# Diagonals of the v rows' weights made one at a time by ScalarE, in a decoder layer on one core

## The chip, the core and the metric

One core of a Trainium2 chip runs the whole layer in one launch. The metric is the device time in microseconds (us), the lower the better. The kernel before takes 3503.22 us, the median of three runs that lie between 3499.84 and 3508.11.

In what follows PE is TensorE (PEld its weight loads), DVE is VectorE, ACT is ScalarE, POOL is GpSimd and SP is SyncE. A line such as L1718 is a line of the kernel before.

## What is computed

The layer has an attention and a convolution branch, and then a PEER channel mixer, which is where the change lies. For each of 1024 tokens PEER picks 128 experts out of 16384 (8 heads, 16 each), takes a row u and a row v of 1024 numbers for each, and adds the v rows up with weights:

```python
    def chunk(xc):
        ...
        u_sel = u_tab[experts]
        act = jax.nn.gelu(jnp.einsum('chkd,cd->chk', u_sel, xc).astype(jnp.float32), approximate=False)
        w = (gates * act).astype(xc.dtype)
        v_sel = v_tab[experts]
        return jnp.einsum('chk,chkd->cd', w, v_sel)
```

The tables are float32, so each token needs 128 u rows and 128 v rows of 4 KB each: 1.07 GB for all tokens.

## The kernel before

The tokens lie in 8 chunks of 128, one token a partition. A first phase projects q, k, v and the convolution's input. In the second phase two things run side by side: the gathers of chunk c, and the front of chunk c + 1 (attention, convolution, the output projection, the queries, the search for the best experts). Its order is written out by hand. A chunk is a pass of 128 slots, and in slot s each engine first does its share of the gathers and then its piece of the front.

The gathers, in slot s of chunk c:

- POOL issues the gather of u row s and that of v row s - 20 (LAG = 20), each an indirect DMA of 128 table rows (512 KB). Each kind has a ring of four buffers (RING = 4), so a gather of u waits for the dot product of the row four before it (`dotted`) and a gather of v for PE's use of the row four before (`row_added`).
- DVE multiplies u row s with the token rows, which lie in PSUM, and sums (L1696, `dot_row`). This gives column s of `dots`.
- ACT takes 16 such columns, a head's, through Gelu (L1530, `gelu`, in slots 0, 16, 32 and so on).
- One slot later (1, 17, 33, ...) DVE multiplies them with the gates (L1708, `weigh_rows`, `weighted`).
- DVE then makes the diagonals: for each row e a 128 x 128 matrix `diag[:, e % 16, :]` with the row's 128 weights on its diagonal and zeros elsewhere. It is the identity times the column of weights. One instruction on 128 x 1024 elements makes eight (L1718, `spread_weights`), in slots 1 and 8 of each 16, so 16 instructions a chunk.
- PE multiplies diagonal and v row and adds into two PSUM banks (L1405, `add_row`, 20 slots behind the dot products). It waits for `diagonal` at every eighth row and for the row's DMA at each.

In chunk 7 five of the last rows (SIDE) are not added by PE but by DVE, after its last dot product (`add_row_aside`, L1727 and L1730).

The front, by slots: attention's eight heads lie in slots 0 to 43, one head in five slots. For each, PE makes the scores, ACT takes them through four activations (L1467 to L1472), DVE runs a scan and a subtraction on each half of the keys (L1603, L1605), ACT an Exp (L1478), PE transposes, ACT copies (L1487) and PE sums (L1363). Beside it DVE does 31 taps of the convolution, four instructions each (L1634). PE's projections follow in slots 49 to 83. The search for the experts is DVE's work alone, in slots 87 to 120 (L1066 to L1166). Chunk 7 has no front beside it.

Chunks 2 to 6 run in a hardware loop on each engine; the others are written out.

## Time and profile before

| | |
|---|---|
| median of three runs | 3503.22 us |
| the profiled execution's own time | 3471.65 us |
| its span | 3469.8 us |
| mean granted clock of TensorE | 0.971 |

The profiled execution is 0.9% below the median of the timed runs. A sum of changes is made against its 3471.65 us and carried over to the median as a difference. What the page calls busy leaves out register and semaphore instructions; POOL's spans are rough. A start or an end of PE's is modelled.

### The profile page before, as it was taken

To read this page: it belongs to the slowest core of one execution; us is meant where nothing else is said; L and a number is where in the kernel's file an instruction comes from. 1 tells how busy PE (TensorE), PEld (TensorE's weight loads), DVE (VectorE), ACT (ScalarE), POOL (GpSimd) and SP (SyncE) were. 2 spreads that over 40 slices of the span, in tenths; PEclk is the share of its full clock that TensorE was granted. 3 is DMA by queue.
4 is the path that set the end of the run, shared out by engine and by line. 5 is a ranking of instruction groups with operands and counts; after the bars stand their busy time and mean duration, and the time that the engine had idled before them with its cause. 6 is when DMAs were issued, how large, how long until landed. Compare 5 with 4: busy or idle time off the path is not lost.

```text
span 3469.8 us, 30029 instructions
## 1 busy us (share of the span) xinstructions
PE 2831.2 (82%) x7929; PEld 1260.8 (36%) x7929; DVE 2348.3 (68%) x5373; ACT 592.7 (17%) x1077; POOL 2027.9 (58%) x2062
## 2 busy tenths in 40 slices
PE   8999488777877998788876988689877988677777
PEld 4445234223432444234432444234432444222222
DVE  2245874987478865988578965978578865944443
ACT  2331210012101420034100420034101420000000
POOL 1000466666666666666666666666666666666664
PEclk9999699999999999999999999999999999999998
DMA  6111899999999999999999999999999999999997
GB/s 217 34 31 58 296 368 353 361 354 361 356 352 362 333 364 344 348 343 354 352 349 346 352 359 352 351 334 354 360 352 343 335 357 353 340 378 372 356 369 279
DMA packets 320480, 1121.68 MB, mean 323 GB/s; under 512 B 36465, under 2 KB 44681, under 8 KB 320296
## 3 DMA queue, kind: packets, MB, share of 16 engines
q0 software_dynamic: 294912, 1073.87, 83.6%
q1 hardware_dynamic: 25384, 45.72, 3.9%
q8 instruction: 71, 1.16, 0.1%
q14 instruction: 113, 0.93, 0.1%
HBM read 1111.01 MB, written 8.45 MB: 323 GB/s over the span
## 4 chain that ended last, share of the span: by engine, by line
PE 22%; DVE 20%; issue 19%; DMA 16%; POOL 7%; another core or an unknown queue 3%; ACT 1%; POOLq 0%; DVEq 0%; ACTq 0%
PE psum L1405 16%; DMA ring_v<-in_peer_v,experts 11%; DVE ring_u L1696 7%; DMA ring_u<-in_peer_u,experts 6%; POOL ring_u L1303 4%; POOL ring_v L1303 4%; DVE acc L1634 2%; PE psum L964 2%; PE psum L1334 1%; PE psum L1363 1%; DVE relu_z L1153 1%; DVE diag L1718 1%; DVE relu_z L1149 1%; PE psum L943 1%
## 5 line engine op out<-in xcount | busy, mean ns | idle before, releaser
L1405 PE MATMUL psum<-ring_v,diag 128*128 128x512 f32 x4076 | 2028.4, 624 | 538.1 <-DMA ring_v<-in_peer_v,experts 455.9
L1696 DVE CUSTOM_DVE_ANT_0 ring_u<-ring_u,psum 128x1024 f32<-128x1024 f32 x1024 | 1241.0, 1215 | 704.0 <-DMA ring_u<-in_peer_u,experts 634.4
L1303 POOL DMA_INDIRECT ring_u<-in_peer_u,experts x1024 | 1005.2, 982 | 797.0 <-DVE experts L1669 351.9
L1303 POOL DMA_INDIRECT ring_v<-in_peer_v,experts x1024 | 1009.0, 985 | 634.1 <-issue 278.8
L1405 PEld LDWEIGHTS psum<-ring_v,diag 128*128 128x128 f32 x4076 | 723.6, 194 | 1589.7 <-DMA ring_v<-in_peer_v,experts 855.6
L478 PE MATMUL psum<-w_sb,xnT 128*128 128x512 f32 x560 | 245.5, 596 | 0.0
L1634 DVE SCALAR_TENSOR_TENSOR acc<-conv_in,taps,acc 128x128 f32<-128x128 f32 x840 | 239.2, 345 | 0.3
L1530 ACT ACTIVATE geld<-dots 128x16 f32<-128x16 f32 x64 | 13.7, 214 | 979.7 <-DVE dots L1696 767.5
L1718 DVE TENSOR_TENSOR diag<-ident,weights 128x1024 f32<-128x1024 f32 x128 | 156.9, 1225 | 7.8 <-issue 2.0
L478 PEld LDWEIGHTS psum<-w_sb,xnT 128*128 128x128 f32 x560 | 106.0, 192 | 126.8 <-issue 123.9
L964 PEld LDWEIGHTS psum<-actT,w_kept 128*128 128x128 f32 x1024 | 130.1, 192 | 52.6 <-issue 46.7
L1603 DVE TENSOR_TENSOR_SCAN log_keep<-log_keep,relu_z 128x512 f32<-128x512 f32 (+1 forms) x96 | 115.7, 1205 | 46.0 <-issue 25.2
L964 PE MATMUL psum<-actT,w_kept 128*128 128x128 f32 x1024 | 131.0, 275 | 4.2 <-ACT actT L1003 4.2
L1334 PE MATMUL psum<-kT,qT 64*128 64x512 f32 (+1 forms) x192 | 108.5, 646 | 7.2 <-DMA qT<-qT_spill 7.2
L943 PE MATMUL psum<-wo_sb,actT 128*128 128x512 f32 x224 | 112.3, 593 | 1.0 <-ACT actT L1523 0.8
L1487 ACT ACTIVATE attT<-psum 128x512 f32<-128x512 f32 (+2 forms) x112 | 58.4, 521 | 311.8 <-PE psum L1350 176.6
L1363 PEld LDWEIGHTS psum<-vals,attT 128*128 128x128 f32 x736 | 94.7, 197 | 34.2 <-issue 33.7
L1363 PE MATMUL psum<-vals,attT 128*128 128x64 f32 x736 | 93.2, 277 | 7.0 <-issue 6.9
L1478 ACT ACTIVATE relu_z<-relu_z 128x512 f32<-128x512 f32 (+1 forms) x96 | 58.2, 608 | 189.6 <-DVE relu_z L1605 142.1
L1350 PE MATMUL psum<-ident,relu_z 128*128 128x128 f32 x368 | 60.1, 277 | 30.7 <-ACT relu_z L1478 22.4
L1696 DVE DVE_READ_ACCUMULATOR2_ANT dots<- 128x1 f32 x1024 | 84.0, 82 | 0.2 <-issue 0.2
L1350 PEld LDWEIGHTS psum<-ident,relu_z 128*128 128x128 f32 x368 | 47.1, 142 | 70.1 <-issue 42.6
(191 smaller groups left out, 1614.6 us busy)
## 6 DMA issues: line engine op xcount, KB each, us to landing
ring_u<-in_peer_u,experts POOLq DMA_INDIRECT x1024
ring_v<-in_peer_v,experts POOLq DMA_INDIRECT x1024
w_sb<-in_w_in SPq DMA_DIRECT2D x4, 2048.0 KB, 19.6
x_in<-in_x SPq DMA_DIRECT2D x8, 512.0 KB, 4.5
w_kept<-in_w_out SPq DMA_DIRECT2D x1, 4096.0 KB, 13.5
h_res<-in_x SPq DMA_DIRECT2D x8, 512.0 KB
w_kept<-in_peer_wq SPq DMA_DIRECT2D x1, 4096.0 KB, 15.2
wo_sb<-in_w_out SPq DMA_DIRECT2D x1, 4096.0 KB, 12.9
```

The costliest lines, as they stand in the source:

```text
L478: last = nc.tensor.matmul(ps[g], xT(i)[:, k, :], w_sb[:, g, k, :], start=k == 0, stop=k == KT_D - 1)
L943: product = nc.tensor.matmul(z[0][:, j * BANK:(j + 1) * BANK], S.actT[:, k, :], wo_sb[:, k, j * BANK:(j + 1) * BANK], start=k == 0, stop=k ...
L964: product = nc.tensor.matmul(z[0][:, h * P:(h + 1) * P], wq_sb[:, k, h * P:(h + 1) * P], S.actT[:, k, :], start=k == 0, stop=k == KT_D - 1)
L1303: nc.gpsimd.indirect_dma_start(ring[kind][:, e % RING, :], None, peer_u[0] if kind == "u" else peer_v[0], bass.IndirectOffsetOnAxis(expert ...
L1334: nc.tensor.matmul(z, qT[lo:lo + HD, a // 2, :], kT[lo:lo + HD, a // 2, lo_key:hi_key], start=True, stop=False)
L1350: last = nc.tensor.transpose(t_ps[:, b * P:(b + 1) * P], S.relu_z[a % 2][:, s:s + P], ident[:, :])
L1363: last = nc.tensor.matmul(o_ps[:, a * HD:(a + 1) * HD], S.attT[:, b, :], vals[:, b, a * HD:(a + 1) * HD], start=n == 0, stop=n == blocks - 1)
L1405: last = nc.tensor.matmul(y_ps[:, j * BANK:(j + 1) * BANK], diag[:, e % TOPK, :], ring["v"][:, e % RING, j * BANK:(j + 1) * BANK], start=F ...
L1603: nc.vector.tensor_tensor_scan(l[:, back], l[:, back], r[:, back], carry, ALU.add, ALU.add).then_inc(S.summed, counts(keys))
L1634: nc.vector.scalar_tensor_tensor(out=acc[:, c, :], in0=conv_in[:, c, t:t + P], scalar=taps[:, c, t:t + 1], in1=acc[:, c, :], op0=ALU.mult, ...
L1696: nc.vector.tensor_tensor_reduce(out=row, in0=row, in1=hn, scale=1.0, scalar=0.0, op0=ALU.mult, op1=ALU.add, accum_out=dots[:, e:e + 1]).t ...
L1718: nc.vector.tensor_tensor(diag[:, at:at + HALF_ROWS, :], spread(ident[:, :], [[0, HALF_ROWS], [1, P]]), spread(weights[:, e:e + HALF_ROWS] ...
```

## The change

ACT makes the diagonals, one a row: 128 a chunk, each the identity through Copy with the row's column of weights as its per-partition scale. Two stand in each of the slots 1 to 8 of every 16. `diagonal` now counts rows, PE waits for it at every row, and each diagonal waits for `row_added` of the row 16 before it, whose place it takes. DVE keeps `weigh_rows`. In chunk 7 the rows of SIDE get no diagonal.

```diff
-    HALF_ROWS = TOPK // 2
+    SPREAD = 1
...
             def add_row(c, e):
 
-                if e % HALF_ROWS == 0:
-                    pe.wait_ge(diagonal, 2 * PH * c + e // HALF_ROWS + 1)
+                is_last = isinstance(c, int) and c == CHUNKS - 1
+                pe.wait_ge(diagonal, pe_rows(e) if is_last else ROWS * c + e + 1)
                 pe.wait_ge(row_in["v"][e % RING], 16 * (FILLS * c + e // RING + 1))
...
+            def spread_weight(c, e):
+
+                is_last = isinstance(c, int) and c == CHUNKS - 1
+                if e % TOPK == 0:
+                    act.wait_ge(weighted, PH * c + e // TOPK + 1)
+                if e >= TOPK or later(c):
+                    act.wait_ge(row_added, pe_rows(e - TOPK) if is_last else ROWS * c + e - TOPK + 1)
+                nc.scalar.activation(diag[:, e % TOPK, :], ident[:, :], ACT.Copy,
+                                     scale=weights[:, e:e + 1]).then_inc(diagonal, 1)
...
+                        h, after = divmod(s, TOPK)
+                        if SPREAD <= after < SPREAD + TOPK // 2 and (h or later(c)):
+                            ch, h = (c, h - 1) if h else (c - 1, PH - 1)
+                            for e in (h * TOPK + 2 * (after - SPREAD), h * TOPK + 2 * (after - SPREAD) + 1):
+                                if not isinstance(ch, int) or ch < CHUNKS - 1 or e not in SIDE:
+                                    spread_weight(ch, e)
...
             gelu(CHUNKS - 1, PH - 1)
+            for e in range(ROWS - TOPK, ROWS):
+                if e not in SIDE:
+                    spread_weight(CHUNKS - 1, e)
...
-                if h or later(c):
-                    dve.wait_ge(diagonal, 2 * (PH * c + h))
+                if later(c):
+                    dve.wait_ge(diagonal, ROWS * (c - 1) + (h + 1) * TOPK)
...
-            def spread_weights(c, e):
-
-                dve.wait_ge(weighted, PH * c + e // TOPK + 1)
-                if isinstance(c, int) and c == CHUNKS - 1 and e == ROWS - HALF_ROWS:
-                    dve.wait_ge(row_added, pe_rows(e - TOPK + HALF_ROWS - 1))
-                elif e >= TOPK or later(c):
-                    dve.wait_ge(row_added, ROWS * c + e - TOPK + HALF_ROWS)
-                at = e % TOPK
-                nc.vector.tensor_tensor(diag[:, at:at + HALF_ROWS, :], spread(ident[:, :], [[0, HALF_ROWS], [1, P]]),
-                                        spread(weights[:, e:e + HALF_ROWS], [[1, HALF_ROWS], [0, P]]),
-                                        ALU.mult).then_inc(diagonal, 1)
...
                             if after == 1:
                                 weigh_rows(ch, h)
-                                spread_weights(ch, h * TOPK)
-                            if after == HALF_ROWS:
-                                spread_weights(ch, h * TOPK + HALF_ROWS)
...
-            spread_weights(CHUNKS - 1, ROWS - TOPK)
             for n, e in enumerate(SIDE):
                 add_row_aside(n, e)
-                if n == 0:
-                    spread_weights(CHUNKS - 1, ROWS - HALF_ROWS)
             end_y()
```

DVE in the loop, slots 97 and 98, before. `u_in2` is the arrival of a u row, `cand` and `top_v` belong to the search.

```order
L1696 ISA ring_u,dots<-ring_u,psum 128x1024 [waits u_in1]
L1696 ISA dots 128x1
L1702 REGISTER_ALU
L1706 REGISTER_ALU [waits gelued]
L1708 TENSOR_TENSOR weights<-geld,gates 128x16 [waits diagonal]
L1716 REGISTER_ALU [waits weighted]
L1718 TENSOR_TENSOR diag<-ident,weights 128x1024 [waits row_added]
L1092 CAST attT<-top_i 128x256 [waits index16]
L1696 ISA ring_u,dots<-ring_u,psum 128x1024 [waits u_in2]
```

The same place after.

```order
L1714 ISA ring_u,dots<-ring_u,psum 128x1024 [waits u_in1]
L1714 ISA dots 128x1
L1720 REGISTER_ALU
L1724 REGISTER_ALU [waits gelued]
L1726 TENSOR_TENSOR weights<-geld,gates 128x16 [waits diagonal]
L1092 CAST attT<-top_i 128x256 [waits index16]
L1714 ISA ring_u,dots<-ring_u,psum 128x1024 [waits u_in2]
```

The instruction of eight diagonals is gone from between the dot product and the search; the multiplication with the gates stays.

ACT in the loop, slots 18 to 20 of the attention, before: the second half's four activations, the copy of the finished chunk to `y_out`, and the Exp of two halves.

```order
L1467 ACTIVATE log_keep_69<-psum 128x512 [waits stick,att_T,z_ready]
L1468 ACTIVATE relu_z_71<-psum 128x512
L1470 ACTIVATE log_keep_69<-log_keep_69 128x512 [waits abs_done]
L1472 ACTIVATE log_keep_69<-log_keep_69 128x512 [waits exp_done]
L1536 REGISTER_ALU [waits row_added]
L1537 ACTIVATE y_out<-psum 128x1024 [waits y_stored]
L1478 ACTIVATE relu_z_71<-relu_z_71 128x512 [waits stick] x2
```

After, from the same activation on.

```order
L1466 ACTIVATE log_keep_69<-psum 128x512 [waits stick,att_T,z_ready]
L1467 ACTIVATE relu_z_71<-psum 128x512
L1469 ACTIVATE log_keep_69<-log_keep_69 128x512 [waits abs_done]
L1471 ACTIVATE log_keep_69<-log_keep_69 128x512 [waits exp_done]
L1538 REGISTER_ALU
L1539 ACTIVATE diag<-ident,weights 128x128 [waits row_added]
L1538 REGISTER_ALU
L1539 ACTIVATE diag<-ident,weights 128x128 [waits row_added]
L1545 REGISTER_ALU [waits row_added]
L1546 ACTIVATE y_out<-psum 128x1024 [waits y_stored]
```

Two diagonals, each with a register operation, now stand ahead of each slot's attention piece; the two shown are those of slot 19.

DVE at the end of chunk 7, before: its weights, eight diagonals, the first row aside, eight diagonals, the other rows aside.

```order
L1708 TENSOR_TENSOR weights<-geld,gates 128x16 [waits diagonal,gelued]
L1718 TENSOR_TENSOR diag<-ident,weights 128x1024 [waits row_added,weighted]
L1727 TENSOR_SCALAR hn_next<-ring_v,weights 128x1024 [waits v_in3]
L1718 TENSOR_TENSOR diag<-ident,weights 128x1024 [waits row_added,weighted]
L1730 SCALAR_TENSOR_TENSOR hn_next<-ring_v,weights,hn_next 128x1024 [waits side_added,v_in3] x4
```

After, these rows read L1726, L1733 and L1736, with no diagonals among them. ACT ends so:

```order
L1529 ACTIVATE geld<-dots 128x16 [waits weighted,dotted]
L1539 ACTIVATE diag<-ident,weights 128x128 [waits row_added,weighted]
L1539 ACTIVATE diag<-ident,weights 128x128 [waits row_added] x11
L1251 UNCONDITIONAL_BRANCH
```

The last eight diagonals no longer stand behind a row aside, which waits for the arrival of its v row.

## Rows read from the trace of the kernel before

**Rows 1.** The page: span, busy time of each engine, DMA.

```profile
span 3469.8 us, 30029 instructions
PE 2831.2 (82%) x7929; PEld 1260.8 (36%) x7929; DVE 2348.3 (68%) x5373; ACT 592.7 (17%) x1077; POOL 2027.9 (58%) x2062
...
DMA  6111899999999999999999999999999999999997
...
q8 instruction: 71, 1.16, 0.1%
q14 instruction: 113, 0.93, 0.1%
```

**Rows 2.** Windows: chunk 4's slots 0-43, 44-87, 88-119, and chunk 7.

```profile
core 0: us, PE busy (x) PEld busy (x) DVE busy (x) ACT busy (x) POOL busy (x), PEclk, DMA share, GB/s
1889.70:2024.51 134.81, 123.06 (x408) 58.03 (x409) 122.22 (x258) 59.96 (x103) 93.37 (x89) 1.00 0.97 357
2024.51:2154.71 130.20, 115.35 (x385) 59.25 (x384) 66.00 (x115) 14.15 (x26) 83.44 (x87) 1.00 0.96 357
2154.71:2251.30 96.59, 68.18 (x131) 23.18 (x129) 91.85 (x275) 3.31 (x5) 63.65 (x66) 0.95 0.94 346
...
3054.36:3420.43 366.07, 261.19 (x511) 89.75 (x510) 175.61 (x280) 2.54 (x8) 241.76 (x252) 0.97 0.96 365
```

**Rows 3.** Windows, L1718 alone (us, DVE busy, clock, DMA): slots 0-43, 88-119.

```profile
1889.70:2024.51 134.81, 7.38 (x6) 1.00 0.97 357
2154.71:2251.30 96.59, 4.89 (x4) 0.95 0.94 346
```

**Rows 4.** Timeline of DVE, chunk 4, slots 97 and 98.

```profile
2187.94 0.17 DVE L1708 TENSOR_TENSOR weights<-geld,gates 128x16 f32<-128x16 f32 x1
2188.24 1.23 DVE L1718 TENSOR_TENSOR diag<-ident,weights 128x1024 f32<-128x1024 f32 x1
2189.38 0.29 DVE L1092 CAST attT<-top_i 128x256 f32<-128x256 uint32 x1
2189.58 1.22 DVE L1696 CUSTOM_DVE_ANT_0 ring_u<-ring_u,psum 128x1024 f32<-128x1024 f32 x1
```

**Rows 5.** Waits of POOL, chunk 4: first slots 0-43, then slots 88-119.

```profile
POOL ring_v L1303 <- PE psum L1405: 10.7, 7, 2.6
POOL ring_u L1303 <- DVE dots L1696: 2.0, 2, 1.7
...
POOL ring_u L1303 <- DVE dots L1696: 9.2, 7, 3.4
POOL ring_u L1303 <- PE psum L1405: 5.5, 2, 3.2
```

**Rows 6.** Groups by form: the removed instruction and ACT's nearest.

```profile
L1718 DVE TENSOR_TENSOR diag<-ident,weights 128x1024 f32<-128x1024 f32 x128 | 156.9, 1225 | 7.8 <-issue 2.0 <-DVE weights L1708 0.5
...
L1509 ACT ACTIVATE actT<-psum,vec 128x128 f32<-128x128 f32 x28 | 8.0, 368 | 34.9 <-remote 19.2 <-PE psum L1385 15.7
...
L1014 ACT ACTIVATE gates_next<-gates_next 128x128 f32<-128x128 f32 x8 | 2.5, 310 | 292.6 <-issue 166.5 <-DVE gates_next L1130 82.8 <-remote 43.3
```

**Rows 7.** Timeline of ACT and DVE, chunk 4, slots 17 to 20.

```profile
1945.19 0.60 ACT L1487 ACTIVATE attT<-psum 128x512 f32<-128x512 f32 x1 [1.56 <-PE psum L1350]
...
1947.31 0.63 ACT L1472 ACTIVATE log_keep<-log_keep 128x512 f32<-128x512 f32 x1
...
1949.46 0.63 ACT L1472 ACTIVATE log_keep<-log_keep 128x512 f32<-128x512 f32 x1
1951.84 1.02 ACT L1537 ACTIVATE y_out<-psum 128x1024 f32<-128x1024 f32 x1 [1.75 <-PE psum L1405]
...
1950.76 1.22 DVE L1603 TENSOR_TENSOR_SCAN log_keep<-log_keep,relu_z 128x512 f32<-128x512 f32 x1
...
1953.75 1.28 DVE L1603 TENSOR_TENSOR_SCAN log_keep<-log_keep,relu_z 128x512 f32<-128x512 f32 x1
```

**Rows 8.** Waits of PE's weight load at the end, 3416 to 3466 us.

```profile
PEld psum L1405 <- DVE diag L1718: 3.8, 1, 3.8
```

**Rows 9.** Timeline of POOL beside DVE, chunk 6, slot 24.

```profile
2740.11 1.97 POOL L1303 DMA_INDIRECT ring_u<-in_peer_u,experts  x1 [0.30 <-issue]
2742.38 0.94 POOL L1303 DMA_INDIRECT ring_v<-in_peer_v,experts  x1 [0.30 <-issue]
...
2740.05 1.22 DVE L1718 TENSOR_TENSOR diag<-ident,weights 128x1024 f32<-128x1024 f32 x1
```

More of the change, by code:

```diff
@@ L1398, in add_row @@
             def add_row(c, e):
-                if e % HALF_ROWS == 0:
-                    pe.wait_ge(diagonal, 2 * PH * c + e // HALF_ROWS + 1)
+                is_last = isinstance(c, int) and c == CHUNKS - 1
+                pe.wait_ge(diagonal, pe_rows(e) if is_last else ROWS * c + e + 1)
                 pe.wait_ge(row_in["v"][e % RING], 16 * (FILLS * c + e // RING + 1))
-                is_last = isinstance(c, int) and c == CHUNKS - 1
                 for j in range(2):
```

## The prediction

> **What bounds the kernel now.** I read the page first, then the stretches of one chunk, then who waits in them. The page says that the 16 DMA engines are busy nine tenths and more from the fifth slice on, that PE is at 82% and DVE at 68% of the span, ACT at 17% [rows 1]. From this alone one would say that the gathers bound everything and that DVE's work is free. The windows say otherwise. Chunk 7, with no front beside it, goes through 128 slots in 366.07 us, 2.86 us a slot, with DVE busy for 175.61 of them: there the gathers set the pace and DVE has slack [rows 2]. Chunk 4, with a front, has three stretches. Slots 0 to 43 take 134.81 us, 3.06 a slot, with DVE busy 91%; slots 44 to 87 take 130.20 us, 2.96 a slot, with DVE busy 51%; slots 88 to 119 take 96.59 us, 3.02 a slot, with DVE busy 95% [rows 2]. DVE is full in the first and the third stretch, and the DMA rate in the third, 346 GB/s, is below chunk 7's 365 [rows 2].
>
> Who sets the pace there is told by POOL, which can issue a gather only when the row four before it is used. In slots 88 to 119 it waited 9.2 us for DVE's dot products and 5.5 us for PE; the dot products follow each other with no gap but their neighbours' work [rows 4, 5]. That stretch is DVE's. In slots 0 to 43 it waited 10.7 us for PE's rows and 2.0 us for DVE's [rows 5]. DVE is full there, but so nearly is PE (123.06 of 134.81 us), and the two are tied to each other through ACT by the attention of each head. That stretch is shared.
>
> **The change part by part.** Removed: 128 instructions of 1.225 us on DVE [rows 6]. They are even through a chunk, 16 in each, but only those in the full stretches count: 6 (7.38 us) in slots 0 to 43 and 4 (4.89 us) in slots 88 to 119 [rows 3].
>
> - Slots 88 to 119. In slot 97 the instruction holds DVE from 2188.24 to 2189.38, 1.14 us, and 0.13 us between the end of the weights and its start go with it [rows 4]. I take 1.2 us, four times, 4.8 us a chunk. The windows allow it: 96.59 less 4.8 is 91.8 us, 2.87 a slot, just above chunk 7's 2.86. I take off a tenth for moments in which a late gather would have stopped DVE anyway: 4.3 us in each of seven chunks (0 to 6), 30 us.
> - Slots 0 to 43. From below nothing, since POOL waits there more for PE; from above all of 7.4 us, since PE's attention pieces wait for DVE's scans. I take half, 3.7 us. Chunk 0 has four such instructions, not six, as it has no weights before slot 17. So 6 x 3.7 and 2.4: 24 us.
> - The others, six in each of those chunks and all 16 of chunk 7: nothing. What hides them is DVE's own slack, 64 of 130 us in the middle stretch and 190 of 366 in chunk 7 [rows 2].
> - The end. PE waited 3.8 us for the last eight diagonals, which stood behind a row aside on DVE [rows 8]. ACT, idle then, makes them directly after the weights. The rows after it are bound by their DMAs in part; I take 3 us, between 0 and 3.8.
>
> Added on ACT: 1019 activations of 128 x 128 from SBUF with a scale per partition. The trace has none of just this kind. The nearest are 310 ns (SBUF, 128 x 128, no scale from memory) and 368 ns (PSUM, with a scale) [rows 6]; I take 340 ns, 5.4 us for each 16, 347 us in all. ACT's share goes from 17% to 27%. In slots 88 to 119 ACT is busy 3.31 of 96.59 us and can't be late [rows 2]. In slots 0 to 43 it is busy 59.96 of 134.81 [rows 2], and 48 diagonals add 16 us. Whether this is late is seen in slots 17 to 20. The two results that DVE's scans need end at 1947.94 and 1950.09, and the scans start at 1950.76 and 1953.75, so there are 2.8 and 3.7 us of slack [rows 7]. Two diagonals (0.7 us) go ahead of the first and four (1.4 us) ahead of the second, and DVE arrives 1.2 us sooner: 0.9 and 1.1 us remain. The copy to `y_out`, for which PE waits at slot 20, had itself waited 1.75 us for PE [rows 7]; six diagonals ahead of it, 2.0 us, use that up. So the chain holds, with little over, and not every slot will be as kind. I take 1 us a chunk, 7 us; from below 0, from above the rival below.
>
> DVE's weights don't wait for ACT's diagonals of the same chunk. ACT now waits at slots 1, 17, ... for `weighted`, and queued behind are its attention pieces of slots 17 and 18. DVE's weights come at the slot's first dot product, and ACT had no earlier work to lose: it was waiting for PE's transposes until 1945.19, at the very time of the weights [rows 7].
>
> Added on PE: a wait at each row instead of each eighth, and a register operation. The diagonal is made at least three slots ahead of its row, as before, and both operations lie ahead of a wait for the row's DMA. Nothing, at most 0.1 us a row where PE streams without a stop.
>
> Added code. In the built program PE's loop body grows from 626 to 834 entries and ACT's from 222 to 479, DVE's shrinks from 786 to 756; with the written-out chunks some 2800 more instructions run. 30029 instructions fetched 2.09 MB [rows 1], 70 bytes each, so 0.2 MB more, 12 packets of 16 KB. One of 16 DMA engines moves 22 GB/s (357 over 16) [rows 2], so a packet takes 0.75 us and can hold up a gather for as long: 9 us at most, I take 6.
>
> **One more term, weighed.** In slot 24 of chunk 6 a gather's issue beside L1718 took 1.97 us, its neighbour 0.94 [rows 9]. One case decides nothing, and I put 0 in the sum; if a third of the 128 cost 1 us each and half of these delayed a gather, it would be 21 us, which the range holds. The Trainium skill (SBUF — State Buffer, "Who interferes with whom" and the summary) says that a DVE operation with two SBUF inputs can block a GpSimd operation that reads SBUF, and that ACT has ports of its own. By that rule the move frees POOL, and the time would be the forecast less those 21 us; the trace agrees in this row.
>
> Against the change speaks another of its rules (Advanced Engine Details and Errata, "The Read-Write Bubble"): ScalarE and VectorE pay a latency between instructions, so use tiles of 512 or 1024 elements. The rows bear this out, since eight times 0.34 is 2.7 us for what took 1.225 [rows 6]. It costs time only where ACT is late, which is the rival below.
>
> **The sum.** -30 - 24 - 3 + 7 + 6 = -44 us. On the profiled execution that is 3471.65 - 44 = 3428 us; on the median 3503 - 44 = 3459 us.
>
> **The rivals.**
>
> - ACT is late in the attention. Speaking for it: the slack of about 1 us that remains in slots 17 to 20 [rows 7], and that ACT works in order, so a late diagonal delays scores, Exp and copies. Against: its 75 idle us in that stretch [rows 2]. If all 48 diagonals land on the chain (16 us a chunk) and only slots 88 to 119 gain (4.3), six chunks lose 11.7 each and the kernel takes 3503 + 70 - 4 (chunk 0) - 3 (the end) = 3566 us. It turns from a gain to a loss at 8.0 us a chunk (4.3 + 3.7), 24 of the 48 diagonals. If it is the case I expect some 34 of them, 11.6 us less 4.3, +44 us, about 3540. Chance 0.10.
> - The gathers take it back. DMA is at 0.94 to 0.97 everywhere [rows 2], and what DVE saves may come back as waits for rows. Against: chunk 7's 2.86 a slot is lower than what remains. It would leave the tail and little else: 3500 us. Chance 0.15.
> - DVE binds the attention too, and POOL is freed. All 7.4 us of slots 0 to 43 (44 in all), 4.8 in slots 88 to 119 (34), 4 at the end and little on the other side: -80 us, 3423. Chance 0.13.
> - The change brings a table load with each group, as Copy stands between Gelu and Exp. The built loop has 12 loads before and after, so this is left at nothing.
>
> My forecast has the remaining 0.62, from 3435 to 3485.
>
> **How the numbers follow.** Within 0.2% (7 us) of the median is what a measurement of this kernel can't tell from no change. Below it lie the forecast (0.62), the third rival (0.13) and a little of the second: 0.76. The second gives the rest, 0.13 for the same. Slower: the first, and a small part of the second, 0.11. The range runs from 3425, near the third rival's 3423, to 3503, the end of no change, and leaves out some 2 in 10.
>
> **What would show it.** DVE's busy time falls by 157 us, ACT's rises by about 350, with a mean near 340 ns. The dot products of slots 97 and 98 lie 1.3 us closer, slots 88 to 119 take about 92 us, and POOL's waits for DVE there shrink. Slots 0 to 43 take about 132 us. Chunk 7 keeps its 366 us. PE's wait for a diagonal at the end is gone. Wrong would be: DVE's scans waiting for ACT's activations by more than a few us a chunk, PE waiting for diagonals or for `y_out`, or the middle stretch growing by what the others lost.

## The result: slower by 0.28%, where 1.3% faster was forecast

The changed kernel takes 3511.14 us (median of 18 runs, 3500.11 to 3520.90), the kernel before 3500.90 us (18 runs, 3488.25 to 3517.53) on the same chip. The ratio is 1.0028, with a 95% interval of 1.0016 to 1.0040. The forecast was 3459 us, its range 3425 to 3503.

The page of the changed kernel: span, busy time of each engine, the sixteen DMA engines in tenths, the two instruction queues, and the chain that ended last.

```profile
span 3507.5 us, 32797 instructions
PE 2820.8 (80%) x7890; PEld 1264.6 (36%) x7929; DVE 2202.5 (63%) x5245; ACT 896.9 (26%) x2096; POOL 1983.5 (57%) x2062
DMA  6111899999999999999999999999999999999998
...
q8 instruction: 73, 1.20, 0.1%
q14 instruction: 137, 1.12, 0.1%
...
PE 22%; DMA 20%; issue 20%; POOL 11%; DVE 10%; another core or an unknown queue 3%; ACT 2%; POOLq 0%; DVEq 0%; ACTq 0%
```

The same chain in the kernel before:

```profile
PE 22%; DVE 20%; issue 19%; DMA 16%; POOL 7%; another core or an unknown queue 3%; ACT 1%; POOLq 0%; DVEq 0%; ACTq 0%
```

VectorE lost 145.8 us of work and ScalarE gained 304.2 [rows 1]: the work moved as the diff says. VectorE's part of the chain that ended last was halved, and the parts of DMA and POOL grew by four points each. The span did not fall. The groups of the same page show where VectorE's time went.

```profile
L1404 PE MATMUL psum<-ring_v,diag 128*128 128x512 f32 x4076 | 2017.6, 621 | 582.4 <-DMA ring_v<-in_peer_v,experts 487.1
L1714 DVE CUSTOM_DVE_ANT_0 ring_u<-ring_u,psum 128x1024 f32<-128x1024 f32 x1024 | 1241.5, 1215 | 848.8 <-DMA ring_u<-in_peer_u,experts 777.0
L1303 POOL DMA_INDIRECT ring_u<-in_peer_u,experts x1024 | 984.9, 962 | 779.8 <-DVE experts L1687 352.9
...
L1539 ACT ACTIVATE diag<-ident,weights 128x128 f32<-128x128 f32 x1019 | 320.4, 388 | 309.6 <-issue 163.5
```

The second row is the dot product. This is its row in the kernel before, and below it the row of the changed kernel in another trace (g1, see below):

```profile
L1696 DVE CUSTOM_DVE_ANT_0 ring_u<-ring_u,psum 128x1024 f32<-128x1024 f32 x1024 | 1241.0, 1215 | 704.0 <-DMA ring_u<-in_peer_u,experts 634.4
...
L1714 DVE CUSTOM_DVE_ANT_0 ring_u<-ring_u,psum 128x1024 f32<-128x1024 f32 x1024 | 1242.5, 1217 | 803.1 <-DMA ring_u<-in_peer_u,experts 730.7
```

VectorE waited for u rows for 634.4 us in the kernel before and 777.0 here, 143 us more. Not all of that is the change's: the trace of the kernel before is of an execution of 3471.65 us and this one of 3509.39, 38 us apart, where the medians differ by 10. g1 took 3477.66 us, and its wait is 96 us longer. In both, time on VectorE turned into waiting on VectorE.

The same stretches as in [rows 2], of the changed kernel: chunk 4's slots 0 to 43, 44 to 87 and 88 to 119, then chunk 7.

```profile
1910.59:2056.64 146.05, 129.30 (x418) 63.22 (x426) 115.77 (x253) 73.56 (x151) 91.04 (x91) 0.95 0.94 338
2056.64:2186.93 130.29, 113.23 (x363) 56.77 (x362) 60.24 (x110) 28.58 (x74) 80.56 (x86) 0.99 0.95 348
2186.93:2282.85 95.92, 67.62 (x134) 24.41 (x132) 87.38 (x270) 13.07 (x37) 61.41 (x64) 0.95 0.97 348
...
3088.29:3460.01 371.72, 261.61 (x513) 91.25 (x512) 157.09 (x265) 42.01 (x135) 236.88 (x253) 0.96 0.95 360
```

VectorE does 4.5 us less in the third stretch, as forecast, but the stretch is only 0.7 us shorter. Chunk 7, in which I expected no change, is 5.7 us longer, and the first stretch 11 us. These are stretches of one chunk in two executions; the table under "Why the prediction was wrong" has all chunks and shows that neither rise is the change's alone. TensorE's granted clock in the first stretch is 0.95, too, where it was 1.00. And yet VectorE's own rows between slots 97 and 98 are as forecast:

```profile
2219.30 0.16 DVE L1726 TENSOR_TENSOR weights<-geld,gates 128x16 f32<-128x16 f32 x1
2219.39 0.28 DVE L1092 CAST attT<-top_i 128x256 f32<-128x256 uint32 x1
2219.59 1.21 DVE L1714 CUSTOM_DVE_ANT_0 ring_u<-ring_u,psum 128x1024 f32<-128x1024 f32 x1
```

From the start of the weights to the next dot product it is 0.29 us, where it was 1.64 [rows 4]: 1.35 us gained in that place. At the end of the stretch most of what four such places gained is gone. The waits of POOL give the first hint of where; the kernel before comes first, the changed kernel second.

```profile
POOL ring_v L1303 <- PE psum L1405: 260.6, 147, 5.1
POOL ring_u L1303 <- DVE dots L1696: 92.2, 91, 4.4
POOL ring_u L1303 <- PE psum L1405: 60.2, 82, 3.5
POOL ring_v L1303 <- remote: 55.5, 25, 4.1
...
POOL ring_v L1303 <- PE psum L1404: 299.6, 148, 5.2
...
POOL ring_v L1303 <- remote: 91.4, 36, 4.1
POOL ring_u L1303 <- DVE dots L1714: 73.8, 81, 4.3
```

Columns: us in total, times, the longest. In both kernels POOL waits nearly 150 times for TensorE's rows ahead of a v gather, over 5 us at the longest, and only 81 to 91 times for VectorE's dot products ahead of a u gather. This was so before the change.

### The profile page after: what moved, and what is told of

It reads as the page before. It is cut to its first block, busy times and chain, and to the rows that moved or that the text cites. A ratio compares the mean times of both kernels' runs of the same rounds, so it can differ in the third digit from the quotient of the medians.

```text
span 3507.5 us, 32797 instructions
## 1 busy us (share of the span) xinstructions
PE 2820.8 (80%) x7890; PEld 1264.6 (36%) x7929; DVE 2202.5 (63%) x5245; ACT 896.9 (26%) x2096; POOL 1983.5 (57%) x2062
## 4 chain that ended last, share of the span: by engine, by line
PE 22%; DMA 20%; issue 20%; POOL 11%; DVE 10%; another core or an unknown queue 3%; ACT 2%; POOLq 0%; DVEq 0%; ACTq 0%
PE psum L1404 16%; DMA ring_v<-in_peer_v,experts 15%; DMA ring_u<-in_peer_u,experts 6%; POOL ring_v L1303 6%; POOL ring_u L1303 5%; DVE ring_u L1714 4%; PE psum L1334 1%; PE psum L943 1%; PE psum L1363 1%; PE psum L964 1%; DVE acc L1652 1%; DVE top_i L1070 1%; DVE relu_z L1073 1%; ACT diag L1539 1%
## 5 line engine op out<-in xcount | busy, mean ns | idle before, releaser
L1714 DVE CUSTOM_DVE_ANT_0 ring_u<-ring_u,psum 128x1024 f32<-128x1024 f32 x1024 | 1241.5, 1215 | 848.8 <-DMA ring_u<-in_peer_u,experts 777.0
L1303 POOL DMA_INDIRECT ring_u<-in_peer_u,experts x1024 | 984.9, 962 | 779.8 <-DVE experts L1687 352.9
L1303 POOL DMA_INDIRECT ring_v<-in_peer_v,experts x1024 | 984.8, 962 | 733.2 <-PE psum L1404 299.6
L1539 ACT ACTIVATE diag<-ident,weights 128x128 f32<-128x128 f32 x1019 | 320.4, 388 | 309.6 <-issue 163.5
L1529 ACT ACTIVATE geld<-dots 128x16 f32<-128x16 f32 x64 | 13.7, 214 | 932.1 <-DVE dots L1714 715.0
```

The costliest lines, as they stand in the source:

```text
L1303: nc.gpsimd.indirect_dma_start(ring[kind][:, e % RING, :], None, peer_u[0] if kind == "u" else peer_v[0], bass.IndirectOffsetOnAxis(expert ...
L1539: nc.scalar.activation(diag[:, e % TOPK, :], ident[:, :], ACT.Copy, scale=weights[:, e:e + 1]).then_inc(diagonal, 1)
L1714: nc.vector.tensor_tensor_reduce(out=row, in0=row, in1=hn, scale=1.0, scalar=0.0, op0=ALU.mult, op1=ALU.add, accum_out=dots[:, e:e + 1]).t ...
```

## The experiments

Eighteen more measurements ran in five sets, each set on one chip beside the kernel before. The chips turned out to differ, so each set names what the kernel before takes on it: 3470.6 us (e), 3265.2 (f), 3466.9 (g), 3261.8 (h), 3470.7 (i). The result above is from a sixth, at 3500.9. I call 3262 to 3265 the quicker chips, the others the slower ones. Ratios are to the kernel before on the same chip unless another kernel is named.

### The parts of the change, one by one (slower chip)

**e1.** TensorE and VectorE skip all diagonals but the first sixteen.

```diff
             def spread_weights(c, e):
+                if later(c) or e >= TOPK:
+                    return
...
-                if e % HALF_ROWS == 0:
-                    pe.wait_ge(diagonal, 2 * PH * c + e // HALF_ROWS + 1)
+                if e % HALF_ROWS == 0 and not later(c) and e < TOPK:
+                    pe.wait_ge(diagonal, e // HALF_ROWS + 1)
```

> Leaves out all diagonals but the first sixteen (the same ones serve every row, so the sums are wrong); no engine makes the others, PE does not wait for them. DVE loses 155 us of work and nothing is added anywhere, the code shrinks a little. Theory D (DVE sets the pace in slots 0 to 43 and 88 to 119, as the forecast had it): 50 to 80 us faster than before, about 3430 to 3450. Theory G (the gathers set the pace everywhere over a stretch of a few slots; DVE's gaps refill as waits for rows): within 10 us of before, 3490 to 3505, and DVE's waits for u rows up by about 150 us.

Measured: 3462.57 us, ratio 0.9984 (0.9969 to 1.0000). VectorE is busy for 2204.9 us as in the changed kernel, and its waits for u rows are 744.0 us. VectorE's relief by itself, with nothing added anywhere, is worth 0.2% here. So most of the forecast gain wasn't eaten by ScalarE's or TensorE's added work: on this chip it wasn't there.

**e2.** ScalarE makes 1008 diagonals into a tile that nobody reads; VectorE's stay. VectorE also waits, once a head, until the sixteen that read the weights it overwrites are made.

```diff
+            def beside(c, e):
+                if e % TOPK == 0:
+                    act.wait_ge(weighted, PH * c + e // TOPK + 1)
+                if later(c) or e > 0:
+                    act.wait_ge(made_aside, ROWS * c + e)
+                nc.scalar.activation(aside[:, :], ident[:, :], ACT.Copy,
+                                     scale=weights[:, e:e + 1]).then_inc(made_aside, 1)
```

> Keeps DVE's diagonals as before and lets ACT make the 128 single ones a chunk as well (but for the last 16), at the same places, into a scratch tile that nobody reads. So it has the change's ACT work and ACT code without its relief of DVE and without PE's waits per row. Theory A (the loss of 10 us comes from ACT being late in the attention, or from its code): 8 to 20 us slower than before. Theory P (the loss comes from PE's waits and PE's code): within 3 us of before.

Measured: 3482.57 us, 1.0029 (1.0014 to 1.0044).

**e3.** TensorE waits at each row; VectorE's instruction counts eight at once.

```diff
-                if e % HALF_ROWS == 0:
-                    pe.wait_ge(diagonal, 2 * PH * c + e // HALF_ROWS + 1)
+                pe.wait_ge(diagonal, ROWS * c + e + 1)
...
-                                        ALU.mult).then_inc(diagonal, 1)
+                                        ALU.mult).then_inc(diagonal, HALF_ROWS)
```

> Before, but DVE's diagonals count by eight and PE waits for its row's count at every row, as after the change. Adds the 96 waits and 112 register operations to PE's loop body, nothing to ACT. Theory P (PE's waits or code cost the 10 us): 8 us or more slower. Theory A: within 3 us of before.

Measured: 3483.57 us, 1.0036 (1.0020 to 1.0051).

**e4.** ScalarE gets two waits a row for what happened long before, and no activations. As in the change, it also waits for `weighted` once in sixteen rows, and that one can be open when ScalarE comes to it.

```diff
+                if e >= TOPK or later(c):
+                    act.wait_ge(row_added, ROWS * c + e - TOPK + 1)
+                act.wait_ge(dotted, ROWS * c + e + 1)
```

> Before, and on ACT at the places of the single diagonals two waits each that have long been fulfilled, with their register operations, but no activation: the added code of ACT and its order of waiting (weights at slot 1 of 16) without the work. If code fetched beside the gathers costs (Theory F), 4 to 10 us slower with 20 or more further packets on the instruction queue; if only ACT's busy time costs (Theory A without the code), within 3 us of before.

Measured: 3475.70 us, 1.0030 (1.0014 to 1.0047); the medians alone differ by 0.15%. The activations of e2 (402.9 us of busy time, 400 ns each) cost no more by these ratios than the waits alone. By the means of twelve runs each, e2 is 3.5 us over e4, a ratio of 1.0010 (0.9994 to 1.0026 by resampling them), so a cost of up to 9 us isn't excluded. In e4's trace ScalarE's queue stands at the wait for `weighted` over 30 times, for 126 us in all, with its attention pieces behind it; no run separates this from the instructions that were added. Each added piece costs some 0.3%, against e1's 0.2%. The pieces don't simply add: e1, e2 and e3 together would be 0.5% slower, and the change is 0.2 to 0.3%.

### Grouped waits, and lighter gathers (quicker chip)

**f1.** The changed kernel, TensorE and ScalarE waiting once in eight rows, four diagonals to a slot.

```diff
-                pe.wait_ge(diagonal, pe_rows(e) if is_last else ROWS * c + e + 1)
+                if is_last and e >= ROWS - LAG:
+                    pe.wait_ge(diagonal, pe_rows(e))
+                elif e % 8 == 0:
+                    pe.wait_ge(diagonal, ROWS * c + min(e + 8, ROWS - LAG) if is_last else ROWS * c + e + 8)
...
-                        if SPREAD <= after < SPREAD + TOPK // 2 and (h or later(c)):
+                        if after in (1, 2, 5, 6) and (h or later(c)):
```

> The changed kernel with its waits taken together: TensorE waits for diagonals once in eight rows, ScalarE waits for added rows once in eight, and makes four diagonals in each of four slots. VectorE still makes none. Against the kernel before. If what the change costs is its added instructions (e3 and e4 each cost 0.3% with waits alone, or nearly), most of that goes and the relief of VectorE stays: ratio 0.998 to 1.001. If the cost is the work of 1024 activations or the handing over from ScalarE to TensorE, it stays at 1.003. If VectorE's relief is worth the 1.2% that I forecast once the waits are out of the way: 0.990.

Measured: 3244.90 us, 0.9938 (0.9923 to 0.9953). I first took this for the groups' doing; g1 and g2 below say otherwise.

**f2.** The kernel before, with 112 more waits a chunk on TensorE, all for the value 1.

```diff
+                else:
+                    pe.wait_ge(diagonal, 1)
```

> The kernel before with the other 112 waits of a chunk on TensorE added as waits for the value 1, fulfilled since the first microseconds, so nothing new is ever waited for and no register is computed for them. If the cost of e3 (0.36%) is that TensorE's stream has more instructions in it: 1.002 to 1.004, with more packets on the instruction queue. If it is that a row waits for a diagonal, or for the arithmetic on the register: 0.999 to 1.001.

Measured: 3266.23 us, 1.0012 (0.9999 to 1.0026): inconclusive, between the two.

**f3 and f4.** Kernel before and changed kernel, with v gathers of half a row; the other half of each place in the ring stays as the first fills left it.

```diff
+                cols = 512 if kind == "v" and (e >= RING or later(c)) else 1024
...
-                    ring[kind][:, e % RING, :], None, peer_u[0] if kind == "u" else peer_v[0],
+                    ring[kind][:, e % RING, 0:cols], None,
+                    peer_u[0] if kind == "u" else peer_v[0] if cols == 1024 else
+                    peer_v[0].rearrange("n (t d) -> (n t) d", t=2),
```

> The kernel before, but each v row's gather fetches 512 of 1024 columns (of other rows; the rest of the ring's row is what the first fills left), so a quarter of the gathered bytes is gone and every instruction stays. If the gathers' bytes bind (the theory that stands after e1): well under the kernel before, 0.90 to 0.96, towards VectorE's and GpSimd's own pace of 2.6 to 2.9 us a slot. If GpSimd's issuing binds and not the bytes: 0.98 to 1.00.

> The changed kernel with the same lighter gathers. To be held against f3. If VectorE's relief was taken back by the gathers' bytes, it shows here: 1.0 to 2.5% under f3 (the 30 to 80 us that VectorE no longer spends where it is the fullest engine), though the change's added instructions cost it 0.3 to 0.6%. If something else than the bytes takes it back (GpSimd's issuing, TensorE's waits): the same as f3 or above it.

Measured: f3 3194.67 us, 0.9774 (0.9752 to 0.9796); f4 3154.32 us, 0.9660 (0.9640 to 0.9680). Between them it is 0.9874 by the medians, 40 us: with lighter gathers the change pays about the 44 us that I had forecast.

### The changed kernel again (slower chip)

**g1** is the changed kernel, **g2** is f1, **g4** is e1. **g3** is the changed kernel with TensorE alone waiting in groups.

```diff
-                pe.wait_ge(diagonal, pe_rows(e) if is_last else ROWS * c + e + 1)
+                if is_last and e >= ROWS - LAG:
+                    pe.wait_ge(diagonal, pe_rows(e))
+                elif e % 4 == 0:
+                    pe.wait_ge(diagonal, min(ROWS * c + e + 4, pe_rows(ROWS - LAG - 1)) if is_last else ROWS * c + e + 4)
```

> The changed kernel itself, once more, beside the kernel before on whatever chip this is: the four light and grouped runs ran on a chip whose kernel before takes 3265 us instead of 3471 to 3501 (382 GB/s in the loop instead of 350). If the ratio of 1.0028 belongs to the change on any chip: 1.002 to 1.004. If quicker transfers let VectorE's relief through, as the lighter gathers did (f4 1.3% under f3): 0.985 to 0.996 on a chip at 3265, and 1.002 to 1.004 on one at 3470 to 3500.

> The grouped kernel of f1 again, beside the changed kernel. If grouping the waits is what brought f1 its 0.9938: 0.5 to 0.8% under g1 on any chip. If it was the chip, and the groups do nothing: the same as g1, within 0.1%.

> The changed kernel with one thing of the grouping: TensorE waits for diagonals once in four rows instead of at each; ScalarE's waits and its slots are as in the change. If the instructions added on TensorE are the cost (e3 0.36% for 112 waits a chunk; 96 of them go here): 0.3% under g1. If ScalarE's are (e4 0.30%): the same as g1, with g2 under both.

> The kernel before with no diagonals made after the first sixteen (e1 again): what VectorE's relief alone is worth on this chip, without any of the change's added work. On a chip at 3470 to 3500: 0.998, as e1. On one at 3265: 0.98 to 0.99 if quicker transfers let the relief through. Either way no kernel that makes its diagonals elsewhere should be under it by more than the interval.

Measured: g1 3473.57 us, 1.0019 (1.0003 to 1.0035). g2 3473.39, 1.0014 (0.9997 to 1.0031). g3 3468.05, 1.0004 (0.9986 to 1.0022). g4 3459.50, 0.9976 (0.9958 to 0.9994). The groups' 0.6% is gone, so it was the chip: g2 and g1 are the same. e1's 0.2% repeats. The change's added work costs 0.4% over g4. g3 is 0.13% under g1, with an interval that reaches zero.

### The quicker kind of chip again

**h1** puts 256 fulfilled waits a chunk on SyncE, **h2** is the changed kernel, **h3** and **h4** are f3 and f4.

```diff
                     store(c - 1)
+                    for e in range(ROWS):
+                        sp.wait_ge(row_added, e + 1)
+                        sp.wait_ge(dotted, e + 1)
```

> The kernel before with 256 waits a chunk that are already fulfilled, on SyncE behind its store of y, where nothing waits behind them but loads needed 300 us later. If e4's 0.3% is what fetching the added code takes from the gathers: 1.002 to 1.004, with more packets on the instruction queues. If it is their place between ScalarE's own work: 0.999 to 1.001.

> The changed kernel on a third chip. If the ratio goes with the speed of the transfers: 1.002 to 1.003 where the kernel before takes 3450 to 3510 us, 0.990 to 0.997 where it takes some 3265. If it doesn't: 1.002 to 1.003 anywhere.

> The kernel before with v gathers of 512 columns. On a chip at 3265 us as f3: 0.977. On one at 3470 to 3500, where more of the time is the gathers': 0.93 to 0.96.

> The changed kernel with the same lighter gathers. If the gathers take VectorE's relief back, then with a quarter of their bytes gone it comes through on any chip: 1.0 to 1.5% under h3, as f4 was under f3 by 1.2%, while h2 beside them stands at 1.002 to 1.003 on a chip at 3470 to 3500. If what lets it through is something else of the quicker chip: 0.2% over h3 on the slower one.

Measured: h1 3261.34 us, 0.9999 (0.9990 to 1.0008). **h2 3239.53, 0.9933 (0.9919 to 0.9946).** h3 3190.67, 0.9783 (0.9764 to 0.9801). h4 3146.34, 0.9647 (0.9634 to 0.9660); h4 to h3 is 0.9861, 44 us. So the same changed kernel is 22 us faster on one chip and 7 to 10 us slower on others. h1 fetched only 3 more packets on its instruction queue than the kernel before (116 against 113), where e4 had fetched 29 more, so it says little on the cost of fetching code.

By now I held that the bytes of the gathers take the relief back, and more so on a chip with slower transfers. The last pair was to show it.

### The theory of the bytes falls (slower chip)

**i1** and **i2** are f3 and f4 with `cols = 256` and `t=4`: v gathers of a quarter row.

> The kernel before with v gathers of 256 of 1024 columns: 37% of the gathered bytes are gone, every instruction stays. On a chip at 3470 to 3500 where the gathers bind: 0.90 to 0.94 (towards some 3180 us, where the half-size gathers brought the quicker chip). On the chip at 3262: 0.970 to 0.978, little under the half-size gathers, since VectorE's and GpSimd's own pace bind there by now.

> The changed kernel with the same gathers. If the bytes take the relief back, it is 1.2 to 1.8% under i1 on any chip: on one at 3470 to 3500 the changed kernel, slower by 0.2 to 0.3% at full bytes, then turns faster. If something else of the slower chips takes it back (their delays in handing over from engine to engine, or fetching the added code): i2 is within 0.3% of i1 there.

Measured: i1 3431.52 us, 0.9898 (0.9881 to 0.9915), where 0.90 to 0.94 was expected. i2 3443.74, 0.9924 (0.9904 to 0.9944); i2 to i1 is 1.0028 by the means of six runs each (1.0012 to 1.0042 by resampling them), where 0.982 to 0.988 was expected. With 37% of the gathered bytes gone the slower chip is hardly quicker, and the change still makes it slower. The page of i1:

```profile
DMA  6111777777767676677777677677767667677775
GB/s 220 34 31 59 267 230 223 225 223 237 230 215 228 222 232 218 217 222 225 224 219 227 217 230 222 216 222 227 223 215 230 215 218 228 218 228 243 229 226 174
```

The DMA engines idle about three tenths of the time, yet chunk 7 takes 359.9 us, against 366.1 with full gathers [rows 2] and 334.8 in h1 with full gathers on the quicker chip.

```profile
2877.71:3212.52 334.81, 254.25 (x514) 87.53 (x512) 175.82 (x281) 2.54 (x8) 245.87 (x253) 0.99 1.02 400
```

## What differs on the slower chips: TensorE's increments arrive late

Laid side by side, chunk 7's slots (from one dot product's start to the next) differ in one thing. On the quicker chip most take 2.56 us, one like the other. On the slower chips the median is 2.56 us as well, but of the 127 slots of the changed kernel 11 take over 4.2 us and 22 more take 3.0 to 4.2; in h2 it is none and 8.

The 2.56 us itself is the gathers' pace. A slot fetches 1.05 MB, in 2.56 us at 410 GB/s, and chunk 7 in h1 ran at 400 GB/s with a DMA share of 1.02. In h2, 93 of the 127 slots take between 2.53 and 2.59 us, with half-row gathers (h4) 6. POOL's own pace is a little quicker: two issues 1.24 us apart, 2.49 us a slot. The changed kernel on the slower chip has 52 slots of 2.53 to 2.59 us, with quarter rows (i1) the kernel before has 13. So bytes set the pace in the undisturbed slots of either chip, and the long slots come on top.

This is one such place in the changed kernel on the slower chip. First TensorE's rows, then POOL's gathers.

```profile
3208.39 1.95 PE L1404 MATMUL psum<-ring_v,diag 128*128 128x512 f32 x4 [0.60 <-issue]
3210.95 1.95 PE L1404 MATMUL psum<-ring_v,diag 128*128 128x512 f32 x4 [0.61 <-DMA ring_v<-in_peer_v,experts]
3213.51 1.95 PE L1404 MATMUL psum<-ring_v,diag 128*128 128x512 f32 x4 [0.61 <-DMA ring_v<-in_peer_v,experts]
...
3210.53 0.94 POOL L1303 DMA_INDIRECT ring_u<-in_peer_u,experts  x1 [0.30 <-issue]
3212.66 0.94 POOL L1303 DMA_INDIRECT ring_v<-in_peer_v,experts  x1 [1.19 <-issue]
3213.91 0.94 POOL L1303 DMA_INDIRECT ring_u<-in_peer_u,experts  x1 [0.31 <-issue]
3218.28 0.94 POOL L1303 DMA_INDIRECT ring_v<-in_peer_v,experts  x1 [3.44 <-PE psum L1404]
```

The v gather at 3218.28 needs the place of the row that TensorE finished at 3212.90 (3210.95 + 1.95). It is issued 5.38 us after that. POOL's wait for `row_added` passed at 3217.51, though the matmuls that count it had long ended. The u gather behind it is held up too, and then TensorE itself runs dry:

```profile
3218.63 1.95 PE L1404 MATMUL psum<-ring_v,diag 128*128 128x512 f32 x4 [0.61 <-DMA ring_v<-in_peer_v,experts]
3222.49 1.96 PE L1404 MATMUL psum<-ring_v,diag 128*128 128x512 f32 x4 [1.90 <-DMA ring_v<-in_peer_v,experts]
3226.26 1.95 PE L1404 MATMUL psum<-ring_v,diag 128*128 128x512 f32 x4 [1.81 <-DMA ring_v<-in_peer_v,experts]
```

The same place of the same kernel on the quicker chip (h2):

```profile
2970.76 1.96 PE L1404 MATMUL psum<-ring_v,diag 128*128 128x512 f32 x4 [0.60 <-DMA ring_v<-in_peer_v,experts]
2973.32 1.96 PE L1404 MATMUL psum<-ring_v,diag 128*128 128x512 f32 x4 [0.60 <-DMA ring_v<-in_peer_v,experts]
...
2973.52 0.94 POOL L1303 DMA_INDIRECT ring_v<-in_peer_v,experts  x1 [0.38 <-DVE dots L1714]
2974.76 0.94 POOL L1303 DMA_INDIRECT ring_u<-in_peer_u,experts  x1 [0.30 <-issue]
2976.09 0.94 POOL L1303 DMA_INDIRECT ring_v<-in_peer_v,experts  x1 [0.38 <-DVE dots L1714]
```

A row ends at 2972.72 and its gather is issued at 2973.52, 0.80 us later; the next ends at 2975.28 and is followed at 2976.09, 0.81 later. POOL's waits for the two rows had passed 0.04 us after their ends.

I worked this out for the first 1000 waits for `row_added` of each profile: when POOL's wait passed, less the later of the row's recorded end and the passing of POOL's wait before it plus 0.57 us, which is its usual distance.

| kernel, chip | over 1 us late | their sum, us | latest, us |
|---|---|---|---|
| before (an execution of 3471.65 us) | 109 | 330 | 4.6 |
| changed (3500.9) | 148 | 451 | 4.8 |
| e1, g4: no diagonals (3470.6, 3466.9) | 144, 130 | 398, 389 | 4.6, 4.8 |
| e2, e3, e4 (3470.6) | 134, 131, 139 | 395, 375, 387 | 4.8, 4.6, 4.7 |
| g1: changed; g2, g3: grouped (3466.9) | 160; 140, 154 | 436; 403, 443 | 4.5; 4.4, 4.7 |
| i1, i2: quarter gathers (3470.7) | 151, 151 | 540, 564 | 7.2, 6.8 |
| f1 to f4, h1 to h4 (3265.2, 3261.8) | none | 0 | 0.3 |

On the quicker chips not one of 8000 waits is late by more than 0.3 us. On the slower ones 11 to 16% are. The trace shows it from the other side too: in i1 three increments of `row_added` stand at 3136.66, 3136.72 and 3136.78, though TensorE's record of a row is 1.95 us long and no two rows start closer than 1.72 us. Increments closer than 0.25 us occur 69 to 125 times a run on the slower chips and never on the quicker. Three in a row occur only with the quarter gathers. VectorE's `dotted` shows one such pair at most, and POOL's waits for it are over 1 us late 21 to 30 times (44 to 73 us in all) on the slower chips and 14 to 16 times (29 to 35 us) on the quicker. So it is TensorE's increments above all. The ends of matmuls are modelled in the trace, so it may be that the row is finished late rather than reported late; for the gather that waits it is the same.

One more thing divides the traces the same way. On the slower chips they hold only 706 to 743 of the 1019 increments of `row_added`, and 18060 to 22581 semaphore updates in all; on the quicker ones none is missing of `row_added`, and it is 42670 to 43567 in all. So the close pairs are counted in an incomplete record. The lateness itself is taken from POOL's waits and TensorE's rows, which are as complete in the one kind as in the other (1016 and 1019). Whether the lost records and the late increments have one cause, and whether the recording has a part in it, no run here can tell.

Late waits and long slots go together. In chunk 7 of the changed kernel on the slower chip, a wait over 1 us late lies at most 8 us before each of the 11 slots of over 4.2 us, and before fewer than half (40) of the 86 slots under 2.7. The lateness there is 68 us in all, and the chunk takes 46.6 us more than 127 slots of 2.56. In h2 there is none, and it takes 9.0 more.

The chips' difference of some 205 us fits in size: 330 to 450 us of lateness with full gathers, a part of which the ring of four rows covers. The sums don't put the kernels in order, though. i1 has 540 us of it and is 39 us quicker than the kernel before, and e1 has more of it than e3 and is 21 us quicker.

That the lateness goes with the chip is shown by traces on four slower chips and two quicker ones. That it is what makes them slower is argued from i1 and from the sums; no experiment took the lateness away. Why it occurs is open.

## Why the prediction was wrong, step by step

One chunk in one execution says little. This table has, from the starts of the dot products, the stretches summed over chunks 0 to 6, and chunk 7, in us. Each line is one trace. e1 and g4 are one kernel, and so are the two changed ones at 3509 and g1: 9 to 11 us between such a pair are no effect.

| kernel (its execution) | slots 0-43 | 44-87 | 88-119 | chunk 7 |
|---|---|---|---|---|
| before (3471.65) | 938.2 | 910.0 | 675.9 | 366.1 |
| changed (3509.39) | 960.5 | 912.0 | 679.9 | 371.7 |
| g1, changed (3477.66) | 949.7 | 901.9 | 677.4 | 364.9 |
| e1, no diagonals (3461.24) | 939.3 | 902.2 | 669.0 | 363.4 |
| g4, no diagonals (3469.44) | 930.4 | 908.4 | 673.6 | 365.6 |
| h1, before, quicker chip (3262.10) | 886.0 | 816.6 | 643.0 | 334.8 |
| h2, changed, quicker chip (3238.18) | 872.3 | 820.2 | 629.3 | 334.1 |

- **Reading what bounds the kernel.** This is the step that failed. I read a DMA share of 0.94 to 0.97 and chunk 7's 2.86 us a slot as the steady pace of the gathers [rows 2]. (The DMA engines are at nine tenths from the sixth slice on, not the fifth [rows 1]; nothing hangs on it.) It is the mean of slots of 2.56 us, which the gathers do set, and of pauses in which POOL waits for a late increment of TensorE's. i1 shows that the bytes are the smaller part: 37% fewer, 6 us less in chunk 7 (on another chip of the slower kind). And I read slots 88 to 119 as VectorE's, from 95% busy and POOL's 9.2 us of waits for it, and so priced the relief at 54 us in two stretches. Measured, the relief alone gives 0.16% and 0.24% on the slower chips, 6 to 8 us (e1, g4). In that stretch VectorE has work queued after a pause and catches up in the next one; a pause that comes from TensorE absorbs what VectorE saves. That last sentence is argued, not measured by itself.
- **-30 us, slots 88 to 119.** On the quicker chip about half of the term is there. The third stretch of chunk 4 in h1 (kernel before, plus SyncE's waits) and in h2 (changed), one below the other:

```profile
2039.89:2131.64 91.75, 65.69 (x133) 22.70 (x132) 91.18 (x275) 3.31 (x5) 62.56 (x64) 0.98 0.98 367
...
2023.74:2112.71 88.97, 65.68 (x134) 22.92 (x132) 86.97 (x271) 13.06 (x37) 61.61 (x64) 0.98 0.99 382
```

  VectorE is busy for 91.18 of 91.75 us there, and the stretch loses 2.8 us; over seven chunks it is 13.7. On the slower chips the change saved nothing there (675.9 us before, 677.4 and 679.9 after), and leaving the diagonals out saved 2 to 7 us, no more than two traces of one kernel differ by.
- **-24 us, slots 0 to 43.** From h1 to h2 it is 13.7 us, a little over half. On the slower chips the changed kernel is over the kernel before here, by 12 us in g1 and 22 in the first trace. On one and the same chip g1 has 19 us more here than g4, which has no diagonals at all, while all of g1 costs 14 to 15 us over g4. So the added work costs most where the attention is, if a single pair of traces can be trusted that far.
- **Nothing elsewhere.** True on the quicker chip, within 4 us in the middle stretch and 1 in chunk 7. On the slower ones too: chunk 7's 5.7 us more in the first trace aren't the change's, since g1 has 364.9 against 366.1.
- **-3 us, the end.** TensorE's weight loads wait for diagonals for 0.5 us in the last 67 us, where they waited 3.8 [rows 8]. The wait went as forecast. From the last dot product to the end it is 47.5 us after 49.4 on the slower chips, but 48.0 after 47.8 on the quicker.
- **+7 us, ScalarE late.** The activation is 388 ns each by the page and 314 ns of busy time (320.4 over 1019), against my 340. e2 costs no more than e4 within the noise, so little of the cost is the activations' own work. But TensorE waits 76.3 us in weight loads and 18.4 us in matmuls for diagonals, for which I had put nothing; in f1, with four diagonals a slot, matmuls wait 2.6 us for them. g2 shows that this made no difference on the slower chip, and in h2, which gains, the two waits are 112.5 and 17.6 us.
- **+6 us, added code, and TensorE's waits at nothing.** Instruction packets rose by 26 and 0.23 MB, the bytes that I had estimated in twice as many packets. What came with them cost more: 0.30% in e4 and 0.36% in e3, some 10 to 12 us each, and 0.4% together. On a quicker chip constant waits, without register operations, cost 0.12% (f2), with an interval from -0.01% to 0.26%. Whether the code, the register operations, the waits or ScalarE's stand at `weighted` cost this on the slower chips isn't settled. The lateness table offers 45 to 65 us more of late increments in e2 to e4 than in the kernel before, but this is one profile each, and e1 has as much more and gains.
- **POOL freed.** POOL's busy time fell from 2027.9 us [rows 1] to 1983.5, 44 us, and a u gather's issue now takes 962 ns in the mean, where it took 982. It goes with VectorE's instructions: POOL is busy for 1996.1 us in e1, which has none of them, and for 2035.7 in e2, which has them and ScalarE's as well. The Trainium skill (SBUF — State Buffer, "Who interferes with whom") says that a VectorE instruction with two SBUF inputs contends with a GpSimd instruction that reads SBUF, and these figures agree with it. Whether the kernel gained anything by it no run shows.
- **The rivals.** "The gathers take it back" gave the nearest time, 3500 us, with a chance of 0.15, and on the quicker chips it is half of the truth: with half-row v gathers the gain goes from 22 to 40 and 44 us. That this meets my sum of 44 is partly luck. By the same sums as in the table, h4 is under h3 by 23.7 us in slots 88 to 119 and by 10.7 in slots 0 to 43, where I had 30 and 24, and by 6.6 in chunk 7, where I had nothing. On the slower chips it is refuted: the relief doesn't come back with 37% of the bytes gone (i2 against i1). The only rival with a loss, ScalarE late in the attention, had +44 us or more from the activations, which e2 against e4 doesn't bear out. None had a cost of ten us for added waits.

## What to carry to other kernels

A DMA share near one doesn't say that bytes bind: look at single slots, and if most run at one pace and every tenth is half as long again, find out whose signal came late before you price a saving by the mean. Take a stretch over all chunks and from two executions before you read 5 us in it. Price a saving on an engine that is full only up to the next pause that it doesn't cause; this last rule is argued here, not shown. Where chips differ by 7%, a change of 1% may change its sign from one to the other; compare on both kinds before keeping it. This change is worth 0.67% on the quicker kind and costs 0.2 to 0.3% on the slower, and waits in groups neither helped nor hurt.

## What the runs showed of the hardware

- Chips of one kind run this kernel at 3262 to 3265 us and others at 3467 to 3501, with equal busy times of the single instructions (dot product 1215 to 1217 ns, matmul 607 to 627 ns at a mean granted clock of 0.98 and 0.97).
- On the slower ones POOL's waits for TensorE's `row_added` pass 1 to 7 us late for some 11 to 16% of the rows, and 27 to 31% of these increments are missing from the trace. On the quicker ones none is over 0.3 us late and none is missing. The cause is unknown.
- Chunk 7's undisturbed slots take 2.56 us, 410 GB/s for 1.05 MB; POOL alone would take 2.49 (h2, h4).
- Some 250 waits a chunk with their register computations, on ScalarE, which idles 83% of the time, cost the whole kernel 0.3% there, or 0.15% by the medians (e4); some of the time at an open wait is in it.
